# One stream of expert rows over all steps, with gathers issued ahead of each step's end

## The chip, the cores and the metric

The kernel runs on one core of a Trainium2 chip, as one launch. The metric is the device time in microseconds, the median of three runs. One core has a TensorE (PE), a VectorE (DVE), a ScalarE (ACT), a GpSimd (POOL), which also issues the gathers, and a SyncE (SP), which issues the other DMAs.

## The reference, cut to what matters

A backbone of two layers works on 128 context tokens and 512 latent tokens of 1024 channels, in float32: five blocks of 128 tokens. In each layer a token goes through four groups of heads (a gated MLP over positions, two attentions over keys, a sliding window), a residual with a layer norm, and then PEER, a feed-forward part made of single experts:

```python
q = (xb @ p['peer_w_q']).reshape(TOKEN_BLOCK, PEER_HEADS, 2, PEER_HALF)
s = jnp.einsum('thpd,pnd->thpn', q, p['peer_sub_keys'], preferred_element_type=jnp.float32)
...
act = jax.nn.gelu(jnp.einsum('thkd,td->thk', p['peer_u'][eid], xb, preferred_element_type=jnp.float32))
return jnp.einsum('thk,thkd->td', (gate * act).astype(xb.dtype), p['peer_v'][eid])
...
x = layer_norm(ALPHA * x + g2 * peer_ffn(x * (1 + sc2) + sh2, p), p['ln2_g'], p['ln2_b'])
```

Each token takes 16 experts in each of 8 heads. So a block needs 128 rows of `peer_u` and 128 of `peer_v` for each of its 128 tokens.

## The kernel before

**Rows.** An expert row of a block is one (kind, head, k): POOL gathers for all 128 tokens the 1024 floats of their own expert into one slot of 128 x 1024 (L502, an indirect DMA). A u row is multiplied by x2 and summed on DVE into `dots` (L603). When 16 u rows of a head are done, ACT takes their gelu (L538) and DVE makes the weights `wsel` (L596). A v row with odd k is then added to `acc` on DVE (L613); one with even k goes through PE (L571) with a diagonal matrix that ACT makes (L545), into `acc_ps` in PSUM. A block is 256 rows. There are 8 slots in `ring`, and in attend and experts-only steps 8 more in `W`. A slot is gathered into again when the row in it has been used.

**Steps.** The program is a sequence of blocks of code that end with a DRAIN on each engine (L683 modulation, L812 input, L1104 attend and route, L1453 experts only, L1485 last sum) and a barrier of all engines (L379), at which semaphores are cleared. For each layer: modulation; input and attend of the context; the four input steps of the latent blocks; the four attend steps of the latent blocks, each of which ends with routing its block's tokens to experts. Experts of a block run inside later steps, between the steps' own instructions. An `Experts` object says which block's heads a step takes:

```python
step_input(L, 1, False, True, Experts(L, 0, 0, 1, begin=True, landings=landings))
...
step_attend_route(L, 2, False, False, Experts(L, 1, 0, PH, begin=True, ended=0, slots=DEEP, landings=landings))
```

In rows per step: each of the four latent input steps 32 (a head of the context's block), the first attend step of the latents 128, each of the other three 256, the modulation of layer 1 64, the input step of its context 32, its attend step 160. Layer 1 ends with a step of 256 rows only and a step with the last sum. In a step with all 8 heads the first 16 u rows come first, then u and v in turn; else 16 u and 16 v in turn.

**Where rows stand in a step.** Each engine's program calls `rows(share)` between its own instructions: do all rows up to that share of 256. POOL's version runs 8 or 16 slots ahead of it, and starts with

```python
gather_until(E.slots)

def rows(share):
    gather_until(E.target(share) + E.slots)
```

so the first gathers of a step are issued at its start. The ids of a head are copied on POOL first (`eid_s`, L493). In an input step POOL calls `rows(96)`, takes a power (L968), does the ropes of the key (L956 to L961), `rows(144)`, a second power (L981), `rows(176)`, the rope of the queries, and `finish()`. DVE makes hT of x (L999) ahead of its first rows.

**The start of a block's experts.** At the start of a step in which a block begins, SP loads ids, the state for the last sum of the block before (four tiles), x2 and gates (L420 to L432), then the attend step's own operands (`xs`, `toep`, `band`, `w_out`, L1110). In an attend step DVE adds `toep` and `band` to the first scores (L1324), and only then does the last sum of the block before (L437 to L440, L405 to L411, with a power on POOL, L446), zeroes `acc` (L465) and starts on rows; PE zeroes `acc_ps` with two matmuls.

Of the kernel before, what the change touches and what calls it, by code (L numbers as in the profile page):

```python
# [61 lines left out]
DIAGS = 4  # L62

# [26 lines left out]
class Experts:  # L90

    def __init__(self, layer, block, first, heads, begin=False, end=False, ended=None, slots=RING, landings=None):
        self.layer, self.block, self.first, self.heads = layer, block, first, heads
        self.begin, self.end, self.ended = begin, end, ended  # L100
        self.order = row_order(heads, 1 if heads == PH else TOPK)

        self.by_dve, self.by_pe = [], []
        d = p = 0
        for kind, _, k in self.order:
# [7 lines left out]
        self.slots = slots  # L113
        self.count = []
        for r in range(len(self.order)):
            landings[r % slots] += 16
            self.count.append(landings[r % slots])

    def target(self, share):

        return min(len(self.order), len(self.order) * share // 256)

    def landed(self, n):

        return self.count[n]


def build(nc, a):
    es = ExitStack()
    with es:  # L130
# [55 lines left out]
        gates_e = sb("gates_e", [P, NSEL])  # L186
        eid_e = sb("eid_e", [P, NSEL], U32)
        eid_s = sb("eid_s", [P, 4, TOPK], U32)
# [158 lines left out]
        ids_in = sem("ids_in")  # L347
        e_in = sem("e_in")
        x2_copied = sem("x2_copied")
        ids_staged = sem("ids_staged")  # L350
        acc_zero = sem("acc_zero")
        used_dve = sem("used_dve")
        used_pe = sem("used_pe")
        gelu_sel = sem("gelu_sel")
        w_ready = sem("w_ready")
        diag_done = sem("diag_done")
# [9 lines left out]
        bias_stored = es.enter_context(nc.semaphore("bias_stored"))  # L366
        gath = [es.enter_context(nc.semaphore(f"gathered{i}")) for i in range(DEEP)]
        landings = [0] * DEEP
# [1258 lines left out]
```

## Time and profile before

| what | us |
|---|---|
| median of three runs | 5282.86 |
| the three runs | 5281.63 to 5284.09 |
| the profiled execution | 5288.38 |
| its span | 5286.6 |
| busy in the span: PE / DVE / POOL / ACT | 3032.0 / 3434.8 / 2815.9 / 633.4 |

The profile is of one execution; its times are counted from the start of the span. In a view, "idle" or a bracket after an instruction is the time for which its engine did nothing before it, with what ended that. `<-DMA band` is a wait for a transfer into `band`. POOLq is the part of POOL that takes instructions in order. The gathers moved 1353.39 MB, the other DMAs 334.49 MB, 320 GB/s over the span.

### The profile page before, as it was taken

The page shows a single profiled execution, that of the slowest core. Times are in us where ns is not written, and L with a number is a line of the kernel's source. Part 1 is how long each engine was busy: PE and PEld are TensorE (multiplying, and loading weights), DVE is VectorE, ACT ScalarE, POOL GpSimd, SP SyncE. Part 2 cuts the span into 40 slices and gives each one's busy share as a digit, 9 for nine tenths or more (in the row PEclk, how much of TensorE's full clock was granted, in tenths as well). Part 3 has the DMA queues.
Part 4 walks back from the last instruction along what each step waited for, and adds up shares of the span by engine and source line. Part 5 has one row for each costly group of instructions (what it writes and reads, how often), then busy time and mean ns, then how long its engine had stood idle before and what let it go on. Part 6 is the DMA issues. An engine that isn't in the chain of part 4 may idle for free. (4 is left out here: it accounts for less than half of the span.)

```text
span 5286.6 us, 34528 instructions
## 1 busy us (share of the span) xinstructions
PE 3032.0 (57%) x9560; PEld 1575.4 (30%) x9560; DVE 3434.8 (65%) x6877; ACT 633.4 (12%) x1577; POOL 2815.9 (53%) x2837
## 2 busy tenths in 40 slices
PE   7638766366356546547554676645554663565354
PEld 1423344134133223311232333423332331332111
DVE  1255467677776866773568555667686677769775
ACT  0101121120121111000110001111111201211000
POOL 1116645366466646644654564445664664665675
PEclk8768868678678767778777786777776886787676
DMA  8447778789899988989896878769898998998998
GB/s 337 159 184 247 250 281 339 292 334 390 309 346 356 352 328 329 393 313 368 325 361 259 307 242 305 286 259 348 343 377 316 337 391 305 339 358 345 355 404 322
DMA packets 439839, 1690.09 MB, mean 320 GB/s; under 512 B 53120, under 2 KB 66496, under 8 KB 427568
## 3 DMA queue, kind: packets, MB, share of 16 engines
q0 software_dynamic: 370528, 1353.39, 67.7%
q1 hardware_dynamic: 69120, 334.49, 16.4%
q8 instruction: 79, 1.29, 0.1%
q14 instruction: 112, 0.92, 0.1%
HBM read 1660.02 MB, written 33.95 MB: 320 GB/s over the span
## 5 line engine op out<-in xcount | busy, mean ns | idle before, releaser
L571 PE MATMUL ps<-ring,diag 128*128 128x512 f32 x1456 | 875.8, 747 | 844.8 <-ACT diag L545 748.7
L502 POOL DMA_INDIRECT ring<-in_peer_u,eid_s x728 | 785.8, 1079 | 596.0 <-DVE dots L603 360.0
L502 POOL DMA_INDIRECT ring<-in_peer_v,eid_s x728 | 737.8, 1013 | 487.1 <-PE ps L571 217.7
L502 POOL DMA_INDIRECT W<-in_peer_v,eid_s x552 | 570.4, 1033 | 349.7 <-issue 125.9
L571 PE MATMUL ps<-W,diag 128*128 128x512 f32 x1104 | 618.8, 698 | 234.2 <-DMA W<-in_peer_v,eid_s 164.6
L603 DVE CUSTOM_DVE_ANT_0 ring<-ring,ps 128x1024 f32<-128x1024 f32 x552 | 658.4, 1217 | 142.4 <-DMA ring<-in_peer_u,eid_s 139.5
L603 DVE CUSTOM_DVE_ANT_0 W<-W,ps 128x1024 f32<-128x1024 f32 x552 | 655.6, 1217 | 102.0 <-DMA W<-in_peer_u,eid_s 100.7
L571 PEld LDWEIGHTS ps<-ring,diag 128*128 128x128 f32 x1456 | 320.7, 235 | 1296.8 <-issue 1126.0
L502 POOL DMA_INDIRECT W<-in_peer_u,eid_s x552 | 540.5, 979 | 292.6 <-DVE dots L603 130.1
L613 DVE SCALAR_TENSOR_TENSOR acc<-ring,wsel,acc 128x1024 f32<-128x1024 f32 x364 | 474.2, 1303 | 99.1 <-DMA ring<-in_peer_v,eid_s 69.5
L613 DVE SCALAR_TENSOR_TENSOR acc<-W,wsel,acc 128x1024 f32<-128x1024 f32 x276 | 354.8, 1286 | 50.0 <-DMA W<-in_peer_v,eid_s 24.7
L571 PEld LDWEIGHTS ps<-W,diag 128*128 128x128 f32 x1104 | 224.3, 218 | 544.2 <-issue 295.8
L869 PE MATMUL ps<-W,hT 128*128 128x512 f32 (+1 forms) x800 | 324.2, 567 | 31.4 <-DVE hT L999 22.1
L1210 PEld LDWEIGHTS ps<-hT,W 128*128 128x128 f32 x2560 | 298.1, 193 | 49.6 <-issue 34.0
L1210 PE MATMUL ps<-hT,W 128*128 128x128 f32 x2560 | 300.6, 277 | 19.4 <-ACT hT L1267 10.4
L545 ACT ACTIVATE diag<-ident,wsel 128x128 f32<-128x128 f32 x640 | 229.0, 398 | 684.6 <-PE ps L571 427.9
L603 DVE CUSTOM_DVE_ANT_0 ring<-ring,x2e 128x1024 f32<-128x1024 f32 x176 | 219.1, 1283 | 87.7 <-DMA ring<-in_peer_u,eid_s 86.7
L493 POOL COPY eid_s<-eid_e 128x16 uint32<-128x16 uint32 x80 | 23.7, 296 | 414.2 <-DMA eid_e<-expert_ids 332.7
L1158 PE MATMUL ps<-ktB,xs 64*128 64x512 f32 x64 | 49.3, 1130 | 331.2 <-DMA xs<-spill_state 202.3
L869 PEld LDWEIGHTS ps<-W,hT 128*128 128x128 f32 x800 | 151.5, 203 | 193.3 <-issue 168.0
L750 PE MATMUL ps<-W,condS 128*2 128x512 f32 x384 | 173.2, 612 | 48.6 <-DMA toep<-in_b_ada 48.6
L1324 DVE SCALAR_TENSOR_TENSOR big<-ps,toep 128x512 f32<-128x512 f32 x32 | 22.1, 689 | 249.9 <-DMA band<-in_c_band 207.4
(212 smaller groups left out, 3311.5 us busy)
## 6 DMA issues: line engine op xcount, KB each, us to landing
W<-in_w_q SPq DMA_DIRECT2D x40, 2048.0 KB
W<-in_w_ada SPq DMA_DIRECT2D x24, 2048.0 KB
W<-in_w_out SPq DMA_DIRECT2D x10, 4096.0 KB, 30.5
W<-in_w_in SPq DMA_DIRECT2D x16, 2048.0 KB, 10.1
ring<-in_peer_u,eid_s POOLq DMA_INDIRECT x728, 6.7
ring<-in_peer_v,eid_s POOLq DMA_INDIRECT x728, 6.3
toep<-mod_rows SPq DMA_DIRECT2D x20, 512.0 KB, 8.7
aux<-mod_rows SPq DMA_DIRECT2D x19, 512.0 KB, 5.7
```

Of the source, the lines that this page charges most:

```text
L493: pool.tensor_copy(eid_s[:, h % 4, :], eid_e[:, ds((E.first + h) * TOPK, TOPK)]).then_inc(ids_staged, 1)
L502: pool.indirect_dma_start(slot(E, r), None, a["peer_u"] if kind == "u" else a["peer_v"], bass.IndirectOffsetOnAxis(ap=eid_s[:, h % 4, k:k ...
L545: act.activation(diag[:, n % DIAGS, :], ident[:, :], ACT.Copy, scale=wsel[:, h % 2, k:k + 1]).then_inc(diag_done, 1)
L571: last = pe.matmul(acc_ps[:, c * 512:(c + 1) * 512], diag[:, (E.by_pe[r] - 1) % DIAGS, :], slot(E, r)[:, c * 512:(c + 1) * 512], start=Fal ...
L603: dve.tensor_tensor_reduce(out=slot(E, r), in0=slot(E, r), in1=x2, scale=1.0, scalar=0.0, op0=ALU.mult, op1=ALU.add, accum_out=dots[:, h % ...
L613: dve.scalar_tensor_tensor(acc[:, :], slot(E, r), wsel[:, h % 2, k:k + 1], acc[:, :], ALU.mult, ALU.add).then_inc(used_dve, 1)
L750: last = pe.matmul(bank(c % NB, parts=2), condS[:, k, :], ada[:, c % NB, k, :], start=(k == 0), stop=(k == KD - 1))
L869: last = pe.matmul(bank(c, n), hT[:, k, :], w_in[c][:, k, :], start=(k == 0), stop=(k == KD - 1))
L1158: pe.matmul(near(i, lat), q, k[:, k0 * P:k0 * P + lat], start=True, stop=True)
L1210: last = pe.matmul(bank(2 + i % 2)[:, g * P:(g + 1) * P], w_q[c][:, k, g * P:(g + 1) * P], hT[:, k, :], start=(k == 0), stop=(k == KD - 1))
L1324: dve.scalar_tensor_tensor(sS[:, i % 2, 0:lat], near(i, lat), sc, bias, ALU.mult, ALU.add)
```

## The change

All rows of all blocks form one `Stream`: for each block 16 u rows, then u and v in turn, and 16 v rows of head 7 last. A step takes a `Slice` of it. A slot is given to the row that follows its least recent user, over steps too; the semaphores that count landings and uses are no longer cleared. POOL's `rows` gathers a row as soon as the row that had its slot lies below the target, up to `limit`, which is 8 or 16 rows past the slice's end: so the first rows of the next step's slice are gathered within this one.

Shares: input steps take 40 rows, the first attend step of the latents 80, the other three 256 (16 v rows of the block before and 240 of their own), modulation 72, the input step of layer 1's context 40, its attend step 160, the experts-only step 272. No rows are taken ahead of the first input step of a layer, nor past the attend step of layer 1's context.

Ids and gates have two buffers, indexed by the block's parity; the copies of ids on POOL go. `acc` is no longer zeroed: the first odd v row writes it with a multiplication, the first even one starts a new sum in PSUM, after the last sum has read the old one. The last sum of a block becomes a generator: one of its parts runs after each row that follows the block's last row, and POOL takes its power behind the 17th gather after it. SP loads x2 and gates ahead of the last sum's tiles. ACT copies x2 to PSUM at the step's start.

```diff
-def row_order(heads, turn):
-    u = [("u", h, k) for h in range(heads) for k in range(TOPK)]
-    v = [("v", h, k) for h in range(heads) for k in range(TOPK)]
-    order, u = u[:TOPK], u[TOPK:]
-    while v:
-        order += u[:turn] + v[:turn]
-        u, v = u[turn:], v[turn:]
-    return order
...
+class Stream:
+    JOB = PH * HEAD_ROWS
+    def __init__(self, jobs):
+        one = [("u", h, k) for h in range(PH) for k in range(TOPK)]
+        two = [("v", h, k) for h in range(PH) for k in range(TOPK)]
+        order = one[:LEAD]
+        for i in range(len(two)):
+            order += one[LEAD + i:LEAD + i + 1] + two[i:i + 1]
+        assert len(order) == self.JOB
+        self.rows = [(j,) + row for j in range(jobs) for row in order]
...
+    def place(self):
+        self.slot, self.landed, self.prev = [], [], []
+        user, count = [-1] * DEEP, [0] * DEEP
+        for i, S in enumerate(self.slices):
+            from_shallow = i == 0 or not self.slices[i - 1].deep
+            for r in range(S.start, S.end):
+                wide = S.deep and not (from_shallow and r < S.start + RING)
+                at = min(range(DEEP if wide else RING), key=lambda n: (user[n], n))
+                self.slot.append(at)
+                self.prev.append(user[at])
+                user[at] = r
+                count[at] += 16
+                self.landed.append(count[at])
...
+        self.limit = min(self.end + ahead, stream.JOB * routed)
...
+        return self.start + self.n * share // 256
...
-        eid_s = sb("eid_s", [P, 4, TOPK], U32)
+        gates_e = sb("gates_e", [P, 2, NSEL])
+        eid_e = sb("eid_e", [P, 2, NSEL], U32)
...
-        acc_zero = sem("acc_zero")
...
+            if S is not None and S.begins is not None:
+                j = S.begins
+                sp.dma_start(eid_e[:, j % 2, :], of_block(eid_dram, JOBS[j][1])).then_inc(ids_in, 16)
+                sp.dma_start(x2e[:, :], of_block(x2_dram, JOBS[j][1])).then_inc(e_in, 16)
+                sp.dma_start(gates_e[:, j % 2, :], of_block(gate_dram, JOBS[j][1])).then_inc(e_in, 16)
+            if S is not None and S.ended is not None and not S.at_end:
+                last_sum_in(sp, *JOBS[S.ended], ended_tiles)
...
+        def last_sum(dve, j, tiles):
             link = chain(dve, end_chain)
-            link(dve.tensor_tensor(acc[:, :], acc[:, :], acc_ps, ALU.add))
+            r = stream.last(j)
+            dve.wait_ge(used_dve, by_dve[r])
+            dve.wait_ge(used_pe, by_pe[r])
+            ins = dve.tensor_tensor(acc[:, :], acc[:, :], acc_ps, ALU.add)
+            ins.then_inc(acc_free, 1)
+            dve.wait_ge(acc_free, j + 1)
+            yield
+            yield
             dve.wait_ge(end_in, 64)
             link(dve.tensor_tensor(acc[:, :], acc[:, :], tiles[1], ALU.mult))
+            yield
             link(dve.scalar_tensor_tensor(acc[:, :], tiles[0], ALPHA, acc[:, :], ALU.mult, ALU.add))
-            layer_norm(link, dve, acc[:, :], tiles[2], tiles[3], tiles[0], st12e, mve, vee[:, :], rstde[:, :],
-                       end_var, end_rstd, 1).then_inc(end_done, 1)
+            yield
+            link(dve.bn_stats(st12e[:, 0, :], acc[:, 0:512]))
+            link(dve.bn_stats(st12e[:, 1, :], acc[:, 512:1024]))
+            link(dve.bn_aggr(mve[:, :], st12e[:, :, :].rearrange("p a n -> p (a n)")))
+            dve.tensor_scalar_add(vee[:, :], mve[:, 1:2], EPS).then_inc(end_var, 1)
+            for _ in range(8):
+                yield
+            dve.wait_ge(end_rstd, 1)
+            link(dve.tensor_scalar(acc[:, :], acc[:, :], mve[:, 0:1], rstde[:, :], ALU.subtract, ALU.mult))
+            yield
+            link(dve.tensor_tensor(acc[:, :], acc[:, :], tiles[2], ALU.mult))
+            yield
+            dve.tensor_tensor(tiles[0], acc[:, :], tiles[3], ALU.add).then_inc(end_done, 1)
+        RSTD_AT = 16
...
-                dve.memset(acc[:, :], 0.0).then_inc(acc_zero, 1)
...
+            def rows(share):
+                t = S.target(share)
+                while pool_at[0] < S.limit and stream.prev[pool_at[0]] < t:
+                    r = pool_at[0]
+                    j, kind, h, k = rows_of[r]
+                    if r == stream.first(j):
+                        pool.wait_ge(ids_in, 16 * (j + 1))
+                    p = stream.prev[r]
+                    if p >= 0:
+                        _, q, _, qk = rows_of[p]
+                        if on_pe(q, qk):
+                            pool.wait_ge(used_pe, by_pe[p])
                         else:
-                            pool.wait_ge(used_dve, E.by_dve[r - E.slots])
+                            pool.wait_ge(used_dve, by_dve[p])
                     pool.indirect_dma_start(
-                        slot(E, r), None, a["peer_u"] if kind == "u" else a["peer_v"],
-                        bass.IndirectOffsetOnAxis(ap=eid_s[:, h % 4, k:k + 1], axis=0)).then_inc(gath[r % E.slots], 16)
-                    at[0] += 1
-            gather_until(E.slots)
-            def rows(share):
-                gather_until(E.target(share) + E.slots)
+                        row_tile(r), None, a["peer_u"] if kind == "u" else a["peer_v"],
+                        bass.IndirectOffsetOnAxis(ap=eid_e[:, j % 2, h * TOPK + k:h * TOPK + k + 1], axis=0)).then_inc(gath[stream.slot[r]], 16)
+                    pool_at[0] += 1
+                    if pow_due[0] and pool_at[0] == stream.last(S.ended) + 1 + RSTD_AT:
+                        pow_due[0] = False
+                        last_sum_rstd(pool)
+            rows(0)
...
-                        if at[1]:
-                            at[1] = False
-                            pe.wait_ge(acc_zero, 1)
-                            for c in range(2):
-                                zeroed = pe.matmul(acc_ps[:, c * 512:(c + 1) * 512], ident[:, :], acc[:, c * 512:(c + 1) * 512],
-                                                   start=True, stop=False, skip_group_check=True)
-                            zeroed.then_inc(acc_zero, 1)
-                        pe.wait_ge(gath[r % E.slots], E.landed(r))
-                        pe.wait_ge(diag_done, E.by_pe[r])
+                        opens = h == 0 and k == 0
+                        if opens and j:
+                            pe.wait_ge(acc_free, j)
...
+                        elif h == 0 and k == 1:
+                            if ending[0] is not None:
+                                for _ in ending[0]:
+                                    pass
+                                ending[0] = None
+                                dve.wait_ge(end_done, 1)
+                            dve.tensor_scalar_mul(acc[:, :], row_tile(r), wsel[:, g % 2, k:k + 1]).then_inc(used_dve, 1)
...
+                    if S.ended is not None and r == stream.last(S.ended) and not S.at_end:
+                        ending[0] = last_sum(dve, S.ended, ended_tiles)
+                    if ending[0] is not None:
+                        next(ending[0], None)
...
-                        if i == 1:
-                            rows(HEAD_MID)
-                            experts_gpsimd_ended(pool, E)
...
+        TAIL_ROWS = TOPK
+        IN_ROWS = 40
+        FIRST_ROWS = Stream.JOB - NLAT * IN_ROWS - TAIL_ROWS
+        MOD_ROWS, CTX_ROWS = TAIL_ROWS + 56, 160
+        def take(n, deep, routed, ahead=RING):
+            return Slice(stream, n, deep, routed, ahead)
+        parts = []
+        for L in range(DEPTH):
+            j = L * NBLK
+            parts += [take(IN_ROWS, False, j + 1) for _ in range(NLAT)]
+            parts.append(take(FIRST_ROWS, True, j + 1, DEEP))
+            parts += [take(Stream.JOB, True, j + b, DEEP) for b in range(2, LAST)]
+            if L + 1 < DEPTH:
+                parts.append(take(Stream.JOB, True, j + LAST))
+                parts.append(take(MOD_ROWS, False, j + NBLK))
+                parts.append(take(IN_ROWS, False, j + NBLK))
+                parts.append(take(Stream.JOB + TAIL_ROWS - MOD_ROWS - IN_ROWS, True, j + NBLK))
+            else:
+                parts.append(take(Stream.JOB, True, j + LAST, DEEP))
+                parts.append(take(Stream.JOB + TAIL_ROWS, True, j + NBLK))
+        assert parts[-1].end == len(stream.rows)
...
-            step_input(L, 1, False, True, Experts(L, 0, 0, 1, begin=True, landings=landings))
+            for b in range(1, NBLK):
+                step_input(L, b, False, b == 1, next(part))
+            step_attend_route(L, 1, False, True, next(part), shares=4)
             for b in range(2, NBLK):
-                step_input(L, b, False, False, Experts(L, 0, b - 1, 1, landings=landings))
-            step_attend_route(L, 1, False, True, Experts(L, 0, NLAT, PH - NLAT, slots=DEEP, landings=landings))
-            step_attend_route(L, 2, False, False, Experts(L, 1, 0, PH, begin=True, ended=0, slots=DEEP, landings=landings))
-            for b in range(2, LAST):
-                step_attend_route(L, b + 1, False, False, Experts(L, b, 0, PH, begin=True, ended=b - 1, slots=DEEP, landings=landings))
+                step_attend_route(L, b, False, False, next(part))
             if L + 1 < DEPTH:
-                step_modulation(L + 1, Experts(L, LAST, 0, 2, begin=True, ended=LAST - 1, landings=landings))
-                step_input(L + 1, 0, True, True, Experts(L, LAST, 2, 1, landings=landings))
-                step_attend_route(L + 1, 0, True, True, Experts(L, LAST, 3, PH - 3, end=True, slots=DEEP, landings=landings))
+                step_modulation(L + 1, next(part))
+                step_input(L + 1, 0, True, True, next(part))
+                step_attend_route(L + 1, 0, True, True, next(part), shares=5)
             else:
-                step_experts_only(Experts(L, LAST, 0, PH, begin=True, ended=LAST - 1, slots=DEEP, landings=landings))
+                step_experts_only(next(part))
```

## Rows read from the trace of the kernel before

**Rows 1.** Windows by step; columns as in the first line.

```profile
core 0: us, PE busy (x) PEld busy (x) DVE busy (x) ACT busy (x) POOL busy (x), PEclk, DMA share, GB/s
1407.00:1864.00 457.00, 246.45 (x824) 134.45 (x824) 331.23 (x655) 62.00 (x152) 262.73 (x267) 0.76 0.91 344
2320.00:2512.00 192.00, 124.53 (x271) 31.36 (x271) 78.60 (x112) 7.38 (x19) 83.73 (x67) 0.82 0.94 372
3006.00:3077.00 71.00, 55.92 (x157) 27.93 (x157) 41.08 (x75) 6.83 (x19) 46.28 (x47) 0.88 0.73 254
4899.00:5256.00 357.00, 185.27 (x260) 60.94 (x260) 244.44 (x339) 27.09 (x74) 261.00 (x265) 0.72 0.99 385
```

**Rows 2.** DVE timeline, attend end and start: start, us, instruction, [idle].

```profile
1399.38 1.28 DVE L613 SCALAR_TENSOR_TENSOR acc<-ring,wsel,acc 128x1024 f32<-128x1024 f32 x1
1400.77 5.45 DVE L613 SCALAR_TENSOR_TENSOR acc<-W,wsel,acc 128x1024 f32<-128x1024 f32 x4
...
1434.98 0.69 DVE L1324 SCALAR_TENSOR_TENSOR big<-ps,toep 128x512 f32<-128x512 f32 x1 [28.77 <-DMA band<-in_c_band]
```

**Rows 3.** DMA queues, 1407.5 to 1435 us.

```profile
q0 software_dynamic: 1407, 5.17, 48.9%
q1 hardware_dynamic: 2028, 4.65, 45.4%
```

**Rows 4.** DVE, then POOL timeline, at two steps' first rows.

```profile
2602.06 1.22 DVE L603 CUSTOM_DVE_ANT_0 ring<-ring,ps 128x1024 f32<-128x1024 f32 x1 [11.37 <-DMA ring<-in_peer_u,eid_s]
...
4929.28 1.01 POOL L502 DMA_INDIRECT ring<-in_peer_u,eid_s  x1 [6.29 <-DVE dots L603]
```

**Rows 5.** Timeline of all engines, 109.8 to 114.6 us.

```profile
110.22 0.82 POOL L647 DMA_DIRECT2D bias_rows<-in_rpb  x1 [28.56 <-issue]
110.41 0.26 DVE L802 COPY modb<-ps 128x96 f32<-128x96 f32 x1 [13.21 <-PE ps L756]
```

**Rows 6.** Line L647, 109 to 115 us: POOL's last DMA there.

```profile
DMA to landing us min/median/max: 3.6/3.6/3.6
```

**Rows 7.** POOL DRAINs: ns min/median/max, first and last start us.

```profile
L683 POOLq DRAIN  x1: 3670/3670/3670, 110.2 to 110.2; - x1
...
L812 POOLq DRAIN  x1: 8114/8114/8114, 3067.4 to 3067.4; - x1
...
L1104 POOLq DRAIN  x1: 5747/5747/5747, 2906.8 to 2906.8; - x1
```

**Rows 8.** Timeline of POOL, then DVE, in the input step from 3006 us.

```profile
3036.33 0.74 POOL L968 TENSOR_TENSOR rstd<-ve,neg_half 128x2 f32<-128x2 f32 x1
...
3068.95 0.94 POOL L502 DMA_INDIRECT ring<-in_peer_v,eid_s  x1 [0.30 <-issue]
...
3011.95 2.64 DVE L999 TENSOR_SCALAR hT<-ps,modb 128x128 f32<-128x128 f32 x8 [7.27 <-PE ps L860]
...
3074.23 1.28 DVE L613 SCALAR_TENSOR_TENSOR acc<-ring,wsel,acc 128x1024 f32<-128x1024 f32 x1 [3.80 <-DMA ring<-in_peer_v,eid_s]
```

**Rows 9.** POOL groups, that step: busy us, mean ns, idle us.

```profile
L502 POOL DMA_INDIRECT ring<-in_peer_u,eid_s x16 | 19.3, 1205 | 5.1 <-issue 4.6 <-POOL eid_s L493 0.5
L502 POOL DMA_INDIRECT ring<-in_peer_v,eid_s x16 | 16.0, 1000 | 11.2 <-PE ps L571 7.0 <-issue 4.0 <-POOL xs L961 0.3
```

**Rows 10.** Line L502 in the input steps of layer 1.

```profile
L502 POOL DMA_INDIRECT ring<-in_peer_u,eid_s x64: 933/943/1996, 2917.1 to 3174.4; - x64
```

**Rows 11.** DVE windows, 128-row attend; then its L603, its L613.

```profile
3237.00:3350.00 113.00, 67.28 (x152) 0.55 0.76 286
3396.00:3455.00 59.00, 32.88 (x48) 0.93 0.99 395
...
3237.00:3350.00 113.00, 37.31 (x64) 0.55 0.76 286
...
3237.00:3350.00 113.00, 6.13 (x5) 0.55 0.76 286
```

More of the change, by code:

```diff
@@ L70 @@
 }
-def row_order(heads, turn):
-    u = [("u", h, k) for h in range(heads) for k in range(TOPK)]
-    v = [("v", h, k) for h in range(heads) for k in range(TOPK)]
-    order, u = u[:TOPK], u[TOPK:]
-    while v:
-        order += u[:turn] + v[:turn]
-        u, v = u[turn:], v[turn:]
-    return order
 def on_pe(kind, k):
     return kind == "v" and k % BY_PE == 0
[L90 to L101, printed above, removed]
+class Stream:
[8 more added lines that the diff above has]
+        self.rows = [(j,) + row for j in range(jobs) for row in order]
         self.by_dve, self.by_pe = [], []
         d = p = 0
-        for kind, _, k in self.order:
+        for _, kind, _, k in self.rows:
             if on_pe(kind, k):
@@ L111, in __init__, with first, last, next_u @@
             self.by_pe.append(p)
[L113 to L117, printed above, removed]
+        self.pe_through = [p for (_, kind, _, k), p in zip(self.rows, self.by_pe) if kind == "v" and k == TOPK - 1]
+        self.slices = []
+    def first(self, j):
+        return j * self.JOB
+    def last(self, j):
+        return (j + 1) * self.JOB - 1
+    def next_u(self, r):
+        while r < len(self.rows) and self.rows[r][1] != "u":
+            r += 1
+        return r
+    def place(self):
[11 more added lines that the diff above has]
+                self.landed.append(count[at])
+class Slice:
+    def __init__(self, stream, n, deep, routed, ahead):
+        self.stream, self.deep = stream, deep
+        self.start = stream.slices[-1].end if stream.slices else 0
+        self.end = self.start + n
+        self.n = n
+        self.limit = min(self.end + ahead, stream.JOB * routed)
+        J = stream.JOB
+        begins = [r // J for r in range(self.start, self.limit) if r % J == 0]
+        ended = [r // J for r in range(self.start, self.end) if r % J == J - 1]
+        assert len(begins) <= 1
+        self.begins = begins[0] if begins else None
+        self.ended = ended[0] if ended else None
+        self.at_end = self.ended is not None and stream.last(self.ended) + 1 == self.end
+        stream.slices.append(self)
     def target(self, share):
-        return min(len(self.order), len(self.order) * share // 256)
-    def landed(self, n):
-        return self.count[n]
+        return self.start + self.n * share // 256
 def build(nc, a):
@@ L1052, in step_input, with step_attend_route @@
             end_step()
[L1055 removed]
+        def step_attend_route(L, b, context, weights, E, shares=8):
             nk = 1 if context else NLAT + 1
@@ L1471, in _ @@
                     rows, finish = experts_gpsimd(pool, E)
-                    experts_gpsimd_ended(pool, E)
+                    for share in range(4, 256, 4):
+                        rows(share)
                     finish()
```

252 lines of the change are left out of this document (115 added, 137 removed).

## The prediction

> **What bounds the kernel.** I read the stretches by step first [rows 1]. No engine is busy throughout. The longest kinds of step are held by DVE and the DMA together: in an attend step with 256 rows (457 us) DVE is busy 331.2 us and the DMA share is 0.91; the experts-only step is at 0.99 of the DMA with 385 GB/s; the modulation step has 0.94. An input step (71 us) is different: DMA 0.73, PE 55.9, DVE 41.1, POOL 46.3, so latencies and the order of work on POOL decide there. An expert row is one gather of 128 x 4 KB = 0.524 MB, issued by POOL. No byte leaves the kernel, so the change can win only stalls at the boundaries between steps and lose only there or on POOL.
>
> Next I read the boundaries. An attend step with 256 rows starts with 28.77 us in which DVE waits for the load of `band` [rows 2], while the two DMA queues share the bandwidth: 5.17 MB of gathers and 4.65 MB of loads go out in 27.5 us [rows 3]. The context's attend of layer 1 waits 11.37 us for its first row, the experts-only step has a hole of 6.29 us on POOL [rows 4]. These are what gathers that are already there could remove.
>
> Then I looked at what a boundary waits for, because the change puts gathers in front of it. At the end of the first modulation every other engine is done at 110.7 (DVE's last copy starts at 110.41 and takes 0.26). POOL issued its last DMA at 110.22 in 0.82 us [rows 5], and that DMA landed 3.6 us after its issue, at 113.8 [rows 6]. POOL's DRAIN at the step's end runs 3.67 us from 110.2, to 113.87 [rows 7]: it ended with the landing, not with the issue at 111.04, and the barrier followed it. The other steps agree. In the input step the last gather's issue ended at 3069.89 [rows 8], its row could start on DVE at 3074.23 because it had landed, and POOL's DRAIN ended at 3067.4 + 8.1 = 3075.5 [rows 7], 5.7 us after POOL's last instruction and after the landing. One row is less clean: the context's attend of layer 1 shows a DRAIN of 5.7 us with no gather left in flight [rows 7], so part of it may be POOL's own tidying. I read this as: **POOL's DRAIN in front of a barrier lets its outstanding gathers land.** Then no gather is in flight over a barrier; those issued ahead have to land before it.
>
> **The input steps (9 of them: eight with latents, one with the context of layer 1).** Today 32 rows, after 40. POOL is the engine in order there: 32 gathers, 35.3 us busy and 16.3 us idle before them, the ropes and two powers between [rows 9]. One gather costs 0.94 + 0.30 us of gap = 1.24 [rows 8]; beside DVE's products it can take up to 2.0 [rows 10]. Before the first power (L968, at 3036.33 [rows 8], 30.6 us into the step) POOL issues 20 gathers today (share 96 of 256 is row 12, and 8 slots). After, the first 8 belong to the step before, so up to share 96 (row 15) it issues 15, each only when a row ahead of it has been used; DVE can begin at 3014.6, when its hT is done, instead of waiting until the first row lands. The power comes 1.5 us sooner. But 40 gathers in all less 15 leaves 25 behind the power, against 12 today: 13 x 1.27 = 16.5 us more on POOL, most of it (13 gathers against 2) behind the last rope, where nothing follows to cover it. Some fills today's waits for PE (7.0 us [rows 9]): I take 4 off. 16.5 - 1.5 - 4 = +11 at the last issue; the landing after it stays in both kernels (5.7 us to the DRAIN's end). Bounds: +5 when nearly all 16.3 us of idle time on POOL is filled, +17 when none is and the gathers meet DVE's products. 9 x 11 = **+99** (45 to 153). The first input step of each layer has 16 gathers more instead of 8 at its end and a longer wait for weights; I leave it at the same price.
>
> **The modulation step**: it moves at 372 GB/s [rows 1], 8 rows more are 4.2 MB, 11.3 us. Its end waits for 8 more landings (+5), its start has 8 rows at hand (-5). **+12** (0 to 22).
>
> **The six attend steps with 256 rows.** Start: with no gather in flight, 4.65 MB of loads alone at 385 GB/s take 12.1 us, plus about 2 before the first lands; broadcast rows may go slower, so I let `band` land at 17 instead of 28.8: -12 (bounds -8 and -14.5). End: DVE's last five rows run from 1399.4 to 1406.2 [rows 2], with as many on PE (they alternate); each frees a slot into which a gather of the next step goes. Ten gathers at 1.24 us from 1400.7 end at 1413; landing and DRAIN add 6 us (as in the input step), so the barrier comes at 1419.5 instead of 1406.5: +13 (bounds +7 and +15). The zeroing of acc (0.9 us) and its matmuls go: -1. The last sum of the block before is the same DVE work in pieces between rows, priced at nothing: DVE's rows cover POOL's power, and without that cover it is 0.7 us. The copies of indices (0.2 us each on POOL) lie in POOL's waits. Sum **0** each, 0 in all (-40 to +45).
>
> **The two attend steps with 128 rows, after 80.** In the attention part (113 us, DVE 67.3) DVE spends 37.31 + 6.13 = 43.4 us on rows (L603 and L613); 37.5% of it is 16 us, of which I count 14, since DVE is the last to be waited for there only part of the time. In the stretch where the query weights load (59 us at DMA 0.99 [rows 11]) a third of the bytes are rows' that now go elsewhere; I take -10, and -5 in the tail. -29, with the end's +13 and -3 at the start (8 gathers fewer against the loads): -19 each, **-38** (-80 to 0).
>
> **The rest.** The context's attend in layer 1: its 11.37 us wait for the first row goes, less a little for the loads that take its place: **-10**. The experts-only step: 16 gathers, 20 us of POOL's pace, are moved to the step before, whose end is priced above; the step is bound by the DMA, so I take **-10** (-20 to 0): the 6.29 us hole and a part of the start.
>
> **Sum.** 99 + 12 + 0 - 38 - 10 - 10 = +53. The profiled execution took 5288.38 us, 1.8 of it outside the span of 5286.6; the median of the runs is 5282.86, 5.5 less, the same differences hold on it: 5283 + 53 = **5336 us**. A change of under 0.2% (10.6 us) can't be told from none.
>
> **A rule that bears on it.** A gather's issue varies between 0.93 and 2.0 us on one and the same tile [rows 10]. The Trainium skill, GPSIMD Engine Reference, "Key points", says that GpSimd shares its SBUF interfaces with VectorE and contends with DVE instructions that have two SBUF inputs. DVE's products in the input steps read both ring and x2e from SBUF, so the long issues agree with it. By the rule, late gathers of the input steps would go at the long figure wherever DVE works beside them, which is the second rival below.
>
> **Rivals.** (1) The DRAIN does not wait for landings, and gathers do stay in flight. For it: the 5.7 us DRAIN with nothing in flight [rows 7]; against it: the first modulation's end. Place: the barriers behind 18 steps (9 input, 8 attend, the modulation); price: 5.7 us each. Inputs +5.3 each (48), modulation +8, attends -8 (loads and gathers now compete) + 7 - 1.3 = -2 each (-14), the 128-row ones -24 each (-48), the rest -20: -26, **5257 us**, faster. It decides when more than half of those 5.7 us are not paid. Chance 0.18. (2) The late gathers of the input steps run beside DVE's products: five of the 13 at 2.0 instead of 0.94 us, +5 in each of nine steps, 45 more: **5381 us**. For it the maximum of 2.0 us; against it the median of 0.94 [rows 10]. Chance 0.15. (3) POOL's idle time swallows the new gathers, so that an input step costs 5, not 11: **5282 us**, the same. For it: 16.3 us idle per step [rows 9]; against it: the idle time lies ahead of the rope, the gathers behind it. Chance 0.12. The forecast has 0.55.
>
> From these: faster by over 0.2% 0.14 (rival 1) + 0.05 (3) + 0.04 (the forecast's lower tail) = 0.23; within 0.2% 0.13; slower 0.64. The likeliest case alone runs from 5295 to 5385. The range that holds 8 in 10 reaches down into rival 1 and up to rival 2: 5235 to 5388.
>
> **What would show it.** Right: at the end of each step with gathers ahead, POOL's DRAIN ends last, some 6 us behind POOL's last gather, and the other engines idle until then; input steps of 80 to 85 us with a run of 13 gathers behind the last rope; attend steps whose first `band` wait is 15 to 18 us instead of 28.8 and whose last gathers start after DVE's last row. Wrong: gathers that land after a barrier, input steps of 75 us or less, or 128-row attend steps shorter by 40 us and more.

## The result, and the profile after

The kernel after takes 5578.48 us (median of 4 runs, 5573.32 to 5582.54) against 5283.48 us for the kernel before on the same chip: ratio 1.0555, 95% interval 1.0537 to 1.0573. It is slower by 295 us. The forecast was 5336 us, slower by 53; the range ended at 5388. The profiled execution has a span of 5580.8 us.

The steps, from one barrier to the next, worked out from the barriers' times in the two profiled executions:

| steps | before, us | after, us | difference | forecast |
|---|---|---|---|---|
| 9 input steps with rows | 687.2 | 926.8 | +239.5 | +99 |
| 6 attend steps, 256 rows | 2737.7 | 2799.1 | +61.4 | 0 |
| modulation of layer 1 | 191.4 | 212.5 | +21.2 | +12 |
| 2 attend steps, 128 rows, now 80 | 614.8 | 599.2 | -15.6 | -38 |
| context's attend, layer 1 | 329.2 | 321.1 | -8.0 | -10 |
| experts only | 356.4 | 352.6 | -3.8 | -10 |

Most of the loss is where it was forecast, in the input steps, but it is 2.4 times as large there; the attend steps with 256 rows add 61 us where none was forecast. Windows of the kernel after, for the steps of [rows 1] (an attend step, the modulation, an input step, experts only):

```profile
core 0: us, PE busy (x) PEld busy (x) DVE busy (x) ACT busy (x) POOL busy (x), PEclk, DMA share, GB/s
1052.00:1519.00 467.00, 250.52 (x820) 138.17 (x820) 329.53 (x654) 63.53 (x154) 270.90 (x259) 0.73 0.90 337
2444.00:2656.00 212.00, 129.57 (x275) 31.32 (x275) 84.09 (x122) 6.89 (x20) 90.41 (x73) 0.81 0.91 357
3193.00:3290.00 97.00, 62.16 (x165) 29.81 (x165) 47.83 (x85) 7.86 (x22) 59.01 (x54) 0.80 0.66 229
5197.00:5549.00 352.00, 199.53 (x288) 65.78 (x288) 253.70 (x347) 28.63 (x81) 253.11 (x257) 0.74 0.99 391
```

In the input step POOL and DVE do more work (59.0 and 47.8 us against 46.3 and 41.1), but the step grew by 26 us, with the DMA share down from 0.73 to 0.66: it waits more. The timeline of POOL in that step (it begins at 3193.1) says where. After it come the last row on DVE and the DRAIN of POOL, with the columns of [rows 7]:

```profile
3202.61 1.69 POOL L546 DMA_INDIRECT ring<-in_peer_u,eid_e  x1 [18.13 <-DVE dots L652]
...
3229.61 0.74 POOL L1022 TENSOR_TENSOR rstd<-ve,neg_half 128x2 f32<-128x2 f32 x1
...
3263.57 0.45 POOL L1015 TENSOR_TENSOR big<-xs,aux 128x128 f32<-128x128 f32 x1
3264.16 0.98 POOL L546 DMA_INDIRECT ring<-in_peer_v,eid_e  x1
...
3281.46 0.94 POOL L546 DMA_INDIRECT ring<-in_peer_v,eid_e  x1 [0.30 <-issue]
...
3277.48 1.28 DVE L665 SCALAR_TENSOR_TENSOR acc<-ring,wsel,acc 128x1024 f32<-128x1024 f32 x1
...
L866 POOLq DRAIN  x1: 10434/10434/10434, 3278.8 to 3278.8; - x1
```

POOL's first gather comes 9.5 us into the step (18.1 us idle before it), when a row has been used. The first power comes at 36.5 us; in the same step before, which starts at 3006.5, it came at 29.8 [rows 8]. The last rope ends at 70.9; 13 gathers follow it; the last is issued by 89.3. DVE used its last row at 85.6 (3278.76). Then nothing goes on but POOL's last three gathers and its DRAIN, which ends at 3278.8 + 10.4 = 3289.2, and the barrier ends the step at 3290.2. (A DRAIN's record starts while gathers ahead of it are still being issued, so its end is what to read.)

The attend steps show the same end. DVE's last row and POOL's last gather of the one that ends at 1519.5, and the DRAIN:

```profile
1504.88 1.28 DVE L665 SCALAR_TENSOR_TENSOR acc<-W,wsel,acc 128x1024 f32<-128x1024 f32 x1
...
1509.86 0.94 POOL L546 DMA_INDIRECT W<-in_peer_v,eid_e  x1 [0.30 <-issue]
...
L1157 POOLq DRAIN  x1: 12373/12373/12373, 1506.2 to 1506.2; - x1
```

DVE is done at 1506.2, the DRAIN at 1518.6. The next attend step then uses `band` at 17.3 us instead of 27.8 [rows 2]:

```profile
1536.78 0.69 DVE L1373 SCALAR_TENSOR_TENSOR big<-ps,toep 128x512 f32<-128x512 f32 x1 [30.61 <-DMA band<-in_c_band]
```

One attend step has this start and not this end: the one before the modulation, which gathers only 8 rows ahead out of its 16 slots. Its last gather and its DRAIN:

```profile
2435.85 0.93 POOL L546 DMA_INDIRECT ring<-in_peer_v,eid_e  x1 [1.93 <-DVE acc L665]
...
L1157 POOLq DRAIN  x1: 7517/7517/7517, 2435.6 to 2435.6; - x1
```

DVE's last row ends at 2442.9, the DRAIN at 2443.1: the slots came free early enough, the landing lies beside DVE's last rows, and the step takes 453.5 us against 456.2 before. In none of the steps with gathers ahead is a gather in flight when POOL's DRAIN ends.

### The profile page after: what moved, and what is told of

It reads as the page before. It is cut to its first block and busy times, and to the rows that moved or that the text cites. A ratio compares the mean times of both kernels' runs of the same rounds, so it can differ in the third digit from the quotient of the medians.

```text
span 5580.8 us, 34531 instructions
## 1 busy us (share of the span) xinstructions
PE 3070.2 (55%) x9520; PEld 1589.4 (28%) x9520; DVE 3415.4 (61%) x6867; ACT 634.7 (11%) x1583; POOL 2890.1 (52%) x2757
## 5 line engine op out<-in xcount | busy, mean ns | idle before, releaser
L618 PE MATMUL ps<-ring,diag 128*128 128x512 f32 x1480 | 970.7, 800 | 886.0 <-ACT diag L598 632.0
L546 POOL DMA_INDIRECT ring<-in_peer_u,eid_e x756 | 786.7, 1041 | 1006.0 <-DVE dots L652 452.3
L546 POOL DMA_INDIRECT ring<-in_peer_v,eid_e x740 | 804.2, 1087 | 707.6 <-PE ps L618 390.3
L546 POOL DMA_INDIRECT W<-in_peer_v,eid_e x540 | 588.2, 1089 | 349.8 <-issue 128.7
L652 DVE CUSTOM_DVE_ANT_0 W<-W,ps 128x1024 f32<-128x1024 f32 x524 | 625.2, 1216 | 118.4 <-DMA W<-in_peer_u,eid_e 117.1
L546 POOL DMA_INDIRECT W<-in_peer_u,eid_e x524 | 537.4, 1026 | 303.4 <-issue 144.0
L652 DVE CUSTOM_DVE_ANT_0 ring<-ring,ps 128x1024 f32<-128x1024 f32 x524 | 627.7, 1216 | 95.6 <-DMA ring<-in_peer_u,eid_e 92.9
L652 DVE CUSTOM_DVE_ANT_0 ring<-ring,x2e 128x1024 f32<-128x1024 f32 x232 | 291.7, 1275 | 136.6 <-DMA ring<-in_peer_u,eid_e 135.8
L1263 PEld LDWEIGHTS ps<-hT,W 128*128 128x128 f32 x2560 | 322.8, 206 | 113.8 <-issue 112.0
L923 PE MATMUL ps<-W,hT 128*128 128x512 f32 (+1 forms) x800 | 309.6, 542 | 14.4 <-DMA W<-in_w_in 11.6
L1399 DVE TENSOR_SCALAR aux<-ps,small 128x64 f32<-128x64 f32 x120 | 34.0, 284 | 246.5 <-PE ps L1231 244.9
```

The costliest lines, as they stand in the source:

```text
L546: pool.indirect_dma_start(row_tile(r), None, a["peer_u"] if kind == "u" else a["peer_v"], bass.IndirectOffsetOnAxis(ap=eid_e[:, j % 2, h * ...
L618: last = pe.matmul(acc_ps[:, c * 512:(c + 1) * 512], diag[:, (by_pe[r] - 1) % DIAGS, :], row_tile(r)[:, c * 512:(c + 1) * 512], start=open ...
L652: dve.tensor_tensor_reduce(out=row_tile(r), in0=row_tile(r), in1=x2, scale=1.0, scalar=0.0, op0=ALU.mult, op1=ALU.add, accum_out=dots[:, g ...
L923: last = pe.matmul(bank(c, n), hT[:, k, :], w_in[c][:, k, :], start=(k == 0), stop=(k == KD - 1))
L1263: last = pe.matmul(bank(2 + i % 2)[:, g * P:(g + 1) * P], w_q[c][:, k, g * P:(g + 1) * P], hT[:, k, :], start=(k == 0), stop=(k == KD - 1))
L1399: dve.tensor_scalar_mul(ob[:, GW + i * HD:GW + (i + 1) * HD], out_of(i), small[:, 48 + i:49 + i]).then_inc(pv_used, 1)
```

## The experiments

Step sums are again from barrier to barrier in each profiled execution; "nine" are the input steps with rows, "six" the attend steps with 256. Compared medians are from runs on the same chip.

**Gathers ahead, or 40 rows?** Three kernels after, with one edit each and with both:

```diff
-            return Slice(stream, n, deep, routed, ahead)
+            return Slice(stream, n, deep, routed, 0)      # ahead0, in32_ahead0
-        IN_ROWS = 40
+        IN_ROWS = 32                                      # in32, in32_ahead0
```

> The kernel after, but no gather is issued for the next step's slice: each step starts with its own first gathers, as before; the stream, the 40 rows, the last sums in parts stay. Theory A (what is issued ahead costs: the gathers for the next step stand at the end of a step, and POOL's DRAIN holds the barrier until they land): DVE's end and the barrier lie within 2 us of each other again, the latent input steps take 80 to 86 us instead of 97 to 101, the attend steps with 256 rows 452 to 460 instead of 466 to 472, and the total is 5310 to 5380. Theory B (the 40 rows of an input step cost, wherever their gathers stand): the input steps stay at 93 or more and the total stays above 5480.

> The kernel after, with 32 rows in an input step instead of 40 (the first latent attend step of a layer then has 112, the context's attend of layer 1 168); gathers ahead stay. Theory A: an input step still ends with 8 gathers ahead and their landing, and loses only the time of 8 rows, some 10 us: 87 to 91 us; the attend steps that take the rows back get 10 to 25 us longer; total 5500 to 5560. Theory B: the input steps fall to 72 to 80 us, total 5380 to 5450.

> Both edits: no gathers ahead and 32 rows in an input step; what is left of the change is the order of rows over the steps, the last sums in parts, no zeroing of acc and no copies of ids. Theories A and B both: input steps at 70 to 76 us, total within 30 us of the kernel before, 5255 to 5315. If it lies above 5350, a third part of the change costs, the order of the rows or the last sums in parts.

| kernel | us | ratio to before | nine | six |
|---|---|---|---|---|
| after | 5578.48 | 1.0555 | +239.5 | +61.4 |
| ahead0 | 5505.33 | 1.0411 (1.0382 to 1.0439) | +150.0 | +67.9 |
| in32 | 5499.01 | 1.0393 (1.0369 to 1.0417) | +121.2 | +56.4 |
| in32_ahead0 | 5434.11 | 1.0264 (1.0240 to 1.0288) | +21.1 | +71.5 |

Neither theory was right alone: both parts cost in the input steps, and they add up. Gathers ahead cost 100 us there without the 8 rows (121.2 - 21.1) and 90 with them (239.5 - 150.0), 10 to 11 per step; the 8 rows cost 129 and 118, 13 to 14 per step. With both undone the nine input steps lose 2.3 us each; no run shows what these are. The six attend steps stayed where they were in all three, and the total of the last was 120 us above the upper end of its expectation: a third part of the change costs.

The price of the gathers ahead in an input step lies behind DVE's last row: the last issues, their landing and the DRAIN. The same input step in in32 (it begins at 3130.7), DVE's last row, POOL's last gather and POOL's DRAIN:

```profile
3203.56 1.28 DVE L665 SCALAR_TENSOR_TENSOR acc<-ring,wsel,acc 128x1024 f32<-128x1024 f32 x1 [2.48 <-DMA ring<-in_peer_v,eid_e]
...
3205.96 0.94 POOL L546 DMA_INDIRECT ring<-in_peer_v,eid_e  x1 [0.30 <-issue]
...
L866 POOLq DRAIN  x1: 10151/10151/10151, 3204.9 to 3204.9; - x1
```

and in in32_ahead0 (it begins at 3093.4):

```profile
3165.61 1.28 DVE L665 SCALAR_TENSOR_TENSOR acc<-ring,wsel,acc 128x1024 f32<-128x1024 f32 x1
...
L866 POOLq DRAIN  x1: 10810/10810/10810, 3156.1 to 3156.1; - x1
```

DVE is done at 74.1 us of the step with gathers ahead and at 73.5 without: having 8 rows at hand at the start made DVE's end no earlier. The DRAIN ends at 84.4 and 73.5.

**How many ahead.** in32 with 4 instead of 8 gathers ahead at the latent input steps:

```diff
-            parts += [take(IN_ROWS, False, j + 1) for _ in range(NLAT)]
+            parts += [take(IN_ROWS, False, j + 1, 4) for _ in range(NLAT)]
```

> The kernel with 32 rows in an input step and gathers ahead, with 4 instead of 8 gathers ahead at the ends of the latent input steps. If the barrier waits for the landing of what is issued ahead (theory A): DVE's last row at the same time as with 8 or none (73.5 to 74.5 us into the step), the last issue some 5 us earlier than with 8, POOL's DRAIN ends at 77 to 81 us and the step takes 78 to 82, between 74.5 (none) and 85.5 (eight). If the slots of the last rows are what holds the last gathers, 4 are free early enough and the step takes 74 to 76.

One run, 5456.43 us. The input step takes 79.6 us, between 74.4 (none) and 85.2 (eight); over the three steps that have 4 ahead at both ends and are alike in layer 1, 79.6 to 81.4. So each gather ahead costs some 1.3 us, near the pace of issues (0.94 + 0.30 us): theory A, as expected. With 8 slots, 4 ahead are not free yet.

**Does the DRAIN wait for landings?** The kernel before with four transfers into free slots at the end of the context's attend step of layer 0, waited for in the next step; once as POOL's gathers, once as SP's loads of the same size:

```diff
+                    if L == 0 and context:
+                        pool.wait_ge(route_done, 2)
+                        for i in range(4):
+                            pool.indirect_dma_start(ring[:, i, :], None, a["peer_u"],
+                                                    bass.IndirectOffsetOnAxis(ap=eid[:, i:i + 1], axis=0)).then_inc(probe, 16)
```

> The kernel before, with four more gathers of 128 x 4 KB that POOL issues at the end of the context's attend step of layer 0, where nothing else is in flight, and that are waited for only in the next step. If POOL's DRAIN waits for landings: its DRAIN ends after the last of the four has landed, 5 to 7 us after that gather's issue, and the step gets 8 to 13 us longer. If it does not wait: the DRAIN ends within 1 us of the last issue, the step gets 3 to 6 us longer, and the gathers land behind the barrier.

> The kernel before, with four more loads of 128 x 4 KB that SP issues at the end of the context's attend step of layer 0, waited for only in the next step: the twin of the probe with POOL's gathers, on SP's queue. If an engine's DRAIN in general waits for its own transfers, SP's DRAIN ends after the last landing and the step gets 8 to 12 us longer. If only POOL's does, the loads land behind the barrier and the step gets 1 to 3 us longer, the time of four issues.

With POOL's gathers the step took 182.8 us instead of 172.8. The last issue, its landing in the line's own view, and the DRAIN:

```profile
341.09 0.93 POOL L1313 DMA_INDIRECT ring<-in_peer_u,eid  x1 [0.30 <-issue]
...
DMA to landing us min/median/max: 4.4/5.6/6.1
...
L1107 POOLq DRAIN  x1: 9076/9076/9076, 338.4 to 338.4; - x1
```

The last issue ended at 342.0, the last gather landed at 341.09 + 6.1 = 347.2, the DRAIN ended at 347.5 and the barrier followed. With SP's loads the step took 174.8 us. SP's issues, the first load of the next step, the landings and SP's DRAIN:

```profile
338.52 1.76 SPq L1152 DMA_DIRECT2D ring<-in_peer_u  x4
341.53 0.33 SPq L421 DMA_DIRECT2D eid_e<-expert_ids  x1
...
DMA to landing us min/median/max: 3.8/5.0/6.3
...
L1107 SPq DRAIN  x1: 122/122/122, 340.3 to 340.3; - x1
```

SP's DRAIN took 0.12 us. The last load landed at 339.85 + 6.3 = 346.2, 4.6 us after the first load of the next step was issued. So POOL's DRAIN waits for what POOL has in flight, and SP's does not wait for SP's.

**The third part.** in32_ahead0, with steps that end where their block's rows end again (tail0), or with the last sum in one piece (lump; in the modulation its power on POOL then also comes some 8 gathers earlier):

```diff
-        TAIL_ROWS = TOPK
+        TAIL_ROWS = 0                       # tail0
...
-                    if S.ended is not None and r == stream.last(S.ended) and not S.at_end:
-                        ending[0] = last_sum(dve, S.ended, ended_tiles)
+            if S.ended is not None and not S.at_end:      # tail0: before the step's first row
+                ending[0] = last_sum(dve, S.ended, ended_tiles)
...
                         ending[0] = last_sum(dve, S.ended, ended_tiles)
+                        for _ in ending[0]:               # lump
+                            pass
```

> The kernel with both edits (no gathers ahead, 32 rows in an input step), and in addition each step again ends with the end of its block's rows, so the rows per step are those of the kernel before and no step starts with 16 v rows of the block before; the last sum of that block runs in parts between the first rows of the next step. It leaves the stream, the parts, no zeroing, no copies of ids. Theory C (the 16 v rows at a step's start cost, since the u rows of the new block are gathered only once these are used): the attend steps with 256 rows go from 466 to 471 back to 454 to 459, the experts-only step from 367 to 354 to 358, the total is 5270 to 5330. Theory D (the last sum in parts costs): the attend steps stay at 464 or more, the total at 5400 or more.

> The kernel with both edits (no gathers ahead, 32 rows in an input step), and the last sum run in one piece right behind the block's last row instead of in parts between rows. Theory C: hardly a change, total 5410 to 5450. Theory D: the attend steps go back to 454 to 459, the modulation to about 195, total 5300 to 5350.

tail0 took 5323.11 us, ratio 1.0071 (1.0054 to 1.0088); lump 5436.16, ratio 1.0284 (1.0267 to 1.0301). The six attend steps went from +71.5 to -4.7 with tail0 and to +84.0 with lump. The 16 v rows of the block before cost, and running the last sum in parts does not. DVE's last row comes 467.1 us into such a step in in32_ahead0, 454.6 in tail0 and 455.3 before (means of the six). Undoing the tail also changes the number of rows in other steps by up to 16, and the experts-only step fell from 367.6 to 345.7, below the 354 to 358 expected. In in32_ahead0 the first u row of the new block is used at 1506.26, 62.9 us into a step that begins at 1443.3:

```profile
1506.26 1.22 DVE L652 CUSTOM_DVE_ANT_0 ring<-ring,ps 128x1024 f32<-128x1024 f32 x1
```

Before, DVE's products began 31.5 us into such a step; in tail0 they begin at 33.8 again (mean of the six). Of the first 16 rows half go to PE when they are v rows, none when they are u rows. So at the same row targets DVE may have done fewer rows while it has time, with more left for the part in which it has none. That is an argument and not shown: how much of the 12.7 us per step this is, and how much the waits of POOL for slots, no run separates.

**The modulation.** Kernel after, with the store of the last sum later in SP's order:

```diff
-                        if c == 1:
+                        if c == 6:
                             experts_sync_ended(sp, E)
```

> The kernel after, with one edit in the modulation: SP waits for the last sum of the block before, and stores it, behind the seventh piece of weights instead of behind the second. If the modulation's 21 us come from SP standing in that wait while pieces of weights are due, the step goes from 212 to 195 to 203 us and the rest is as in the kernel after (total some 5565). If they come from the 8 more rows and their landing, it stays at 209 or more.

The modulation fell from 212.5 to 196.9 us (one run, total 5559.54). In the kernel after, SP issues nothing from 2486.4 to 2538.1: it stands in the wait for the last sum, which is ready only when enough rows have been used, while pieces of weights are due:

```profile
2486.13 0.25 SPq L750 DMA_DIRECT2D toep<-in_b_ada  x1
2538.06 0.35 SPq L506 DMA_DIRECT2D x_state<-aux  x1
```

Before, the same store was issued at 2365.1, 44 us into the step; here it is 94 us in.

**Versions that beat both.** The kernel before, with the operands of the scores issued ahead of the last sum's tiles, x2 and gates (loads_first), and in addition with w_out issued behind the first four heads (loads_first_w):

```diff
-                    experts_sync(sp, E)
+                    if E is not None and E.begin:
+                        sp.dma_start(eid_e[:, :], of_block(eid_dram, E.block)).then_inc(ids_in, 16)
...
                         lay(band[:, :], a["c_band"][:, ds(NLAT * P - b * P, lat)], x_loaded)
+                    if E is not None and E.begin:
+                        experts_sync_rest(sp, E)
...
-                    lay(W[:, 0:KD * D], a["w_out"][L, :, :], loaded2)
...
                     sp.wait_ge(negmax, H)
+                    lay(W[:, 0:KD * D], a["w_out"][L, :, :], loaded2)      # loads_first_w
```

> The kernel before, with one edit: in the attend steps SP issues the operands of the scores (qT, qTC, toep, band) ahead of the tiles of the last sum, x2 and gates, only the ids stay first. The wait for band at the start of six steps falls from 28 to 14 to 17 us. If the start sets the step's length: 10 to 13 us each, total 5205 to 5225. If the DMA gives the time back later in the step, where weights and rows share it, as the kernel after shows (10.5 us at the start, 1.3 us left behind the routing): 0 to 3 us each, total 5265 to 5285.

> The kernel before with the operands of the scores loaded first, and the 4 MB of w_out, first used some 200 us later, issued only behind the first four heads' scores. If rows early in the step wait for bandwidth that w_out takes, the attend steps lose 3 to 8 us more against the version with the operands first alone: total 5230 to 5255. If the DMA is the bound over the whole step, nothing more is won: 5260 to 5275.

loads_first took 5268.10 us, ratio 0.9962 (0.9949 to 0.9974); loads_first_w 5263.58, ratio 0.9948 (0.9932 to 0.9965). Both are faster than the kernel before, by 0.4 and 0.5%, and than the kernel after; moving w_out added nothing that the two intervals tell apart. DVE's wait for `band` in loads_first:

```profile
1415.29 0.69 DVE L1333 SCALAR_TENSOR_TENSOR big<-ps,toep 128x512 f32<-128x512 f32 x1 [11.89 <-DMA band<-in_c_band]
```

The step begins at 1404.4, so band is used at 10.9 us instead of 27.8. The six attend steps became 17.1 us shorter in all, 2.9 each, of 17 won at the start. The total is that of the expectation's second case, but its reason, a DMA that gives the time back later in the step, is not what the trace shows. Most of the gain is gone at once. ACT's first work in a step is to copy x2 to PSUM, and x2 and the gates now land behind the operands of the scores. DVE's first row waits for that copy, and so does the first head's exponential, which stands behind it on ACT:

```profile
1430.34 1.02 ACT L528 COPY ps<-x2e 128x1024 f32<-128x1024 f32 x1 [43.17 <-DMA gates_e<-gate_state]
1431.29 0.82 ACT L1259 ACTIVATE big<-big,small 128x640 f32<-128x640 f32 x1
...
1431.39 1.22 DVE L609 CUSTOM_DVE_ANT_0 ring<-ring,ps 128x1024 f32<-128x1024 f32 x1 [12.34 <-ACT ps L528]
```

In the kernel before the same copy started 14.4 us into the step, here 26.0. The first head's exponential came 2.8 us earlier than before, where `band` came 16.9 earlier. So what was won was the wait for `band`; a wait for x2 took its place.

## Why the prediction was wrong

- **POOL's DRAIN lets its gathers land**: right. The probe with four gathers shows it, and the attend steps that gather 16 rows ahead pay 12.4 us between DVE's end and the DRAIN's end, forecast 13. Rival 1, gathers that stay in flight, is out.
- **The input steps**: this is the step that failed. The sum 16.5 - 1.5 - 4 = +11 per step should have been +26.6. Its mechanism, POOL in order with gathers behind the last rope, was right, and 13 gathers behind the rope is what the trace has. What failed is the time of the last issue: in the step shown it came 25.9 us later (89.3 us into the step against 63.4) instead of 11. Term by term, worked out from POOL's timelines of that step before and after:
  - "The power comes 1.5 us sooner" is wrong: it came 6.7 us later (36.5 against 29.8; 6.2 in the mean of the nine). The term took the 15 gathers ahead of the power at the pace of issues, but they run from 9.5 to 36.5 us, 1.8 us each, because a ring of 8 refills only as rows are used. It also counted on DVE no longer waiting for its first row to land; before, DVE did not wait for it either, as its first row started at 3014.50, right behind hT (line below).
  - 13 x 1.27 = 16.5 behind the power is too small: the 13 more gathers took 20.6 there, and the ropes and the second power between them took 2.0 more.
  - "I take 4 off" for waits that are filled behind the power held (3.5). The idle time that grew lies ahead of the power: in all, POOL's idle time before gathers went from 16.3 us [rows 9] to 29.9 within the step. The groups below add up to 38.5, of which 8.6 lie in the step before, behind its last gather.
  - "The landing after it stays in both kernels" nearly held: from the last issue's end to the DRAIN's end it is 5.7 us before and 6.9 after.

  The gathers ahead (10 to 11 us a step) and the 8 rows (13 to 14) were each about as dear as the whole term.

```profile
3014.50 1.22 DVE L603 CUSTOM_DVE_ANT_0 ring<-ring,x2e 128x1024 f32<-128x1024 f32 x1
```

```profile
L546 POOL DMA_INDIRECT ring<-in_peer_u,eid_e x20 | 23.6, 1179 | 26.4 <-DVE dots L652 20.9 <-issue 5.5
L546 POOL DMA_INDIRECT ring<-in_peer_v,eid_e x20 | 22.3, 1114 | 12.1 <-PE ps L618 7.4 <-issue 3.7 <-DVE dots L652 0.3
```

- **Rival 2**, slow issues beside DVE's products: it happened in part, inside the second of the two wrong terms. Over the whole step the mean issue was 1.18 and 1.11 us, 1.21 and 1.00 before [rows 9], but behind the power it rose from 1.01 to 1.15: seven of the 25 issues there took 1.30 to 1.98 us, where one of 12 was long before. That is some 4 us of the step; the rival had put it at 5, all of it in the gathers behind the last rope. The Trainium skill (GPSIMD Engine Reference, "Key points") says that GpSimd shares its SBUF interfaces with VectorE and contends with DVE instructions that have two SBUF inputs. The trace agrees: all seven ran beside a row on DVE that reads two tiles of SBUF, as below, though not every issue beside one was long (0.95 us at 3268.53).

```profile
3259.08 1.98 POOL L546 DMA_INDIRECT ring<-in_peer_u,eid_e  x1 [0.30 <-issue]
...
3259.02 1.22 DVE L652 CUSTOM_DVE_ANT_0 ring<-ring,x2e 128x1024 f32<-128x1024 f32 x1
```

- **Rival 3**, idle time that swallows the gathers: the opposite, it grew.
- **The attend steps with 256 rows**: forecast 0, measured +10.2 each. The start gained 10.5 (forecast 12) and the end lost 12.4 (forecast 13), and these two do about cancel: with gathers ahead the six steps are 1.1 us shorter each than without (ahead0), 2.5 with 32 rows (in32 against in32_ahead0). The gain at the start was carried to the end: DVE's last row comes 455.2 us into the step after, 466.5 in ahead0 (means of the six). What failed is a term put at nothing: the 16 v rows of the block before cost 12.7 us (in32_ahead0 against tail0, 76.2 over six). The line shows the last row on DVE in a step of ahead0 that begins at 998.4: it ends 466.7 us into the step. In the same step of the kernel after, which ends at 1519.5, the last row ends at 454.2 us.

```profile
1463.82 1.28 DVE L665 SCALAR_TENSOR_TENSOR acc<-W,wsel,acc 128x1024 f32<-128x1024 f32 x1
```

- **The attend steps with 80 rows**: -7.8 each instead of -19. Without the DRAIN's wait for gathers ahead (ahead0) it is -21.4.
- **The modulation**: +21.2 instead of +12. The term missed is SP's stand in the wait for the last sum, 15.7 of it (mod_store). That the last sum in pieces between rows costs nothing is true of DVE in the attend steps (lump) and not of SP, whose order has that wait in front of weights.

## What to carry to other kernels

Before a transfer is issued ahead over a barrier, look at which engine issues it: what is in POOL's queue is waited for at POOL's DRAIN, so its landing is added to the end of the step unless its slot comes free a landing's time before the step's last work; a load on SP's queue goes through. With a ring that refills as rows are used, a gather moved out of a step's start into the end of the step before was no gain in the input steps, where the engine that issues it works in order: the start idles and the end is exposed; in the attend steps gain and loss about cancelled. The order of rows was priced at nothing and cost 12.7 us a step there. When a result gets ready later, look through every engine's order for a wait on it, the queues' as well: the work behind that wait is what it costs. A load that is moved up moves others down: in loads_first 12 of the 17 us won at `band` were lost at once to x2, which an engine in order wanted first.

## What the runs showed of the hardware that was not expected

SP's DRAIN and POOL's differ: SP's took 0.12 us with four loads of 0.5 MB in flight, POOL's ended 5.5 us behind the last issue of four gathers of the same size.

POOL's DRAIN does more than wait for the last landing. In the input step shown the last gather landed at 3287.6 and the DRAIN ended at 3289.2, 1.7 us later; in the probe it was 0.3 us. The time between grows with the number of gathers of the step (from the traces of all kernels here, those with gathers ahead and those without):

| gathers in the step | 4 | 32 | 40 | 48 | 64 | 72 | 88 |
|---|---|---|---|---|---|---|---|
| from last landing to the DRAIN's end, us | 0.30 | 1.35 | 1.67 | 2.0 | 2.66 | 2.98 | 3.64 |

That is 0.041 us per gather, and the value for 32 is 1.35 or 1.36 in all 86 such steps. It does not go on like this: attend steps with 256 gathers show 2.49. So the DRAIN of 5.7 us with nothing in flight [rows 7], behind 160 gathers that had landed 35 us before it began, does not speak against the wait for landings: it fits work of POOL's own on gathers that have landed. What that work is the traces do not show.
